# Storing the activated products of two neighbouring table blocks by one transfer in a Hyena, GLA and PEER layer

## The chip, the cores and the metric

The kernel runs on one NeuronCore of a Trainium2 chip. The metric is device time in microseconds (us) of one execution on that core. All data are 32-bit floats; the large products run as float32r matmuls on split operands (a high and a low part), three matmuls for each product.

## The reference, cut to what matters

The layer is computed for 640 tokens: 128 of a prompt and 512 of a sample. The part that matters here is the expert channel mixer at its end. Each token is given 8 x 16 = 128 of 16384 experts; its output is the sum of their rows of a value table, weighted by a gate times the gelu of the token's product with their rows of a key table.

```
    def block(args):
        xt, it, gt = args
        a = jax.nn.gelu(jnp.einsum('td,tkd->tk', xt, u_tab[it]))
        return jnp.einsum('tk,tkd->td', gt * a, v_tab[it])
```

Before it stand the norms, the input projection, the long convolution, the chunked linear attention, the output projection and the product-key search for the 128 experts; the change touches none of them.

## The kernel before, in words

The 640 tokens are five tiles of 128. For three of them (384 tokens, `TA`), the kernel computes the product of every token with every row of the key table `u`, densely, in 128 blocks of 128 table rows, and takes the gelu of it; a dense matrix of gates (zero where an expert is not chosen) later picks what counts. For the two other tiles the chosen rows of `u` are gathered by indirect DMA (`gather_u`, issued by POOL, four buffers `ugat`) and multiplied on DVE (`dot`). Everything goes through DRAM scratch between the two halves: the activated products through `gelu_scratch` (`a_dram`), the gates through `gate_scratch` (`g_dram`).

The dense blocks are numbered n = 0 to 127. For each one:

- SP loads 512 KB of the table into one of four buffers `uraw` (`load_u`), four blocks ahead.
- ACT writes the high part `uhi` (`split_u`), two buffers; POOL (up to block 52) or DVE (after it) writes the low part `ulo`, two buffers.
- PE does 24 matmuls (`first_products`) into one of four PSUM banks.
- ACT takes the gelu from the bank into one of four buffers `aout` (`gelu`), and counts `gelu_done`.
- SP stores the 192 KB of `aout` to `a_dram` (`store_a`), which counts one of the semaphores `a_stored`. Gelu of block n + 4 waits for it, since it writes the same buffer.

SP works strictly in the order of its program: for block n it waits for gelu n, stores, waits for `uhi` and `ulo` of block n, and loads block n + 4. There are three stretches of such blocks. In stretch A (blocks 0 to 51) DVE does the search for the experts beside them. In stretch B (blocks 52 to 115, 64 blocks, `step_b`) PE does eight more matmuls per block that make the gate matrix of 128 tokens from one-hot vectors, ACT copies it to `gst`, and after every eighth block SP stores half of it in two parts of 2048 KB (`store_g`): part 0 right behind block b = 7 or 15 of the sixteen, part 1 behind the store and the load of the next block. Beside this DVE does about 2.8 dots per block up to block 96, two after that, each on a gathered 512 KB. In stretch C (blocks 116 to 127) there are no more gates; DVE does one dot per block, and SP puts in the first four loads of the value table (`load_2`, 512 KB each) and the first read-back of activations and gates (`load_gates(0)`, 768 and 1024 KB, behind block 122). After it stretch D runs the 128 blocks of the second product, 24 matmuls of 512 columns each, for which the activations, gates and value rows are loaded by SP.

All DMAs of SP stand in one queue (q1 of the profile), POOL's gathers in another (q0); both run on the core's 16 DMA engines.

Names and lines: `load_u` L545, `store_a` L549 to L552, `step_a` L558, `store_g` L570, `step_b` L576, stretch C on SP L616 to L632, `first_products` L934 to L951 (its matmuls are L947), ACT's `split_u` L1730 (the activation is L1738), `gelu` L1744, DVE's `dot` L1473 (the operation is L1478), POOL's `gather_u` L1881 (L1886).

Of the kernel before, what the change touches and what calls it, by code (L numbers as in the profile page):

```python
# [127 lines left out]
def bass_hybrid_layer(nc, x, cvec, w_ada, w_in, w_out, w_q, cols, hfcols, hf_w1, hf_w2, hf_w3,  # L128
                      gla_w2, gnorm, state, keys_t, u_t, u_rows, v_tab, zfeat, decay, tab_fwd, tab_inv, tab_p,
                      masks, ident_d, iota_d, out, out_state):  # L130
    a_dram = nc.dram_tensor("gelu_scratch", [P, NBLK, TA], F32, kind="Internal").ap()
# [4 lines left out]
    with ctx:  # L136
        base = 16 * KiB + 256

        def at(name, kib, shape, dt=F32):
            return nc.alloc_sbuf_tensor_at(name, shape, dt, offset=int(base + kib * KiB))  # L140

        def sem(name):
            return ctx.enter_context(nc.semaphore(name))
# [61 lines left out]
        aout = at("aout", 112, [P, 4, TA])  # L205
# [227 lines left out]
        s2_used = sem("s2_used")  # L433
        y_tile = sem("y_tile")
        g_stored = [sem(f"g_stored{b}") for b in range(2)]
        a_stored = [sem(f"a_stored{b}") for b in range(4)]
        u_landed = [sem(f"u_landed{b}") for b in range(4)]
        uhi_ready = sem("uhi_ready")
        ulo_ready = sem("ulo_ready")
# [1 line left out]
        gelu_done = sem("gelu_done")  # L441
# [43 lines left out]
        def _(sp_):  # L485
# [59 lines left out]
            def load_u(n, slot):  # L545
                sp_.dma_start(uraw[:, slot], u_t[bass.ds(n, 1)].rearrange("o p k e -> p (o k) e")
                              ).then_inc(u_landed[slot], 16)

            def store_a(n, slot):  # L549
                sp_.wait_ge(gelu_done, n + 1)  # L550
                sp_.dma_start(a_dram[:, bass.ds(n, 1), :].rearrange("p o t -> p (o t)"), aout[:, slot]
                              ).then_inc(a_stored[slot], 16)  # L552

            wait_unit(sp_, last_unit(loads[-3]))
            for n in range(4):
# [2 lines left out]
            def step_a(it, first):  # L558
                for b in range(4):
                    n = it * 4 + b  # L560
                    store_a(n, b)
                    sp_.wait_ge(uhi_ready, n + 1)
                    sp_.wait_ge(ulo_ready, n + 1)
                    load_u(n + 4, b)
# [32 lines left out]
            def load_2(n):  # L597
                b = n % R2
                if n >= R2:
                    sp_.wait_ge(vhi_ready, n - R2 + 1)  # L600
                    sp_.wait_ge(vlo_ready, n - R2 + 1)
                sp_.dma_start(vraw[b][:], v_tab[n * P:(n + 1) * P, :]).then_inc(v_landed[b], 16)

            def load_gates(m):

                if m >= 2:
                    sp_.wait_ge(w_ready, R2 * (m - 1))
                sp_.dma_start(ain[m % 2][:].rearrange("p i t -> p (i t)"),
                              a_dram[:, R2 * m:R2 * (m + 1), :].rearrange("p i t -> p (i t)")).then_inc(a_landed[m % 2], 16)
                if m >= 2:  # L610
                    sp_.wait_ge(wlo_ready, R2 * (m - 1))
                sp_.dma_start(gin[m % 2][:].rearrange("p c i t -> p c (i t)"),
                              g_dram[:, :, R2 * m:R2 * (m + 1), :].rearrange("c p i t -> p c (i t)")).then_inc(g_landed[m % 2], 16)

            for n in range(BLK_C, NBLK):
                store_a(n, n % 4)  # L616
                if n + 4 < NBLK:
                    sp_.wait_ge(uhi_ready, n + 1)
                    sp_.wait_ge(ulo_ready, n + 1)
                    load_u(n + 4, n % 4)  # L620
                if n == BLK_C + 2:
                    sp_.wait_ge(gate_staged, TD // 4)
                if BLK_C + 2 <= n < BLK_C + 2 + R2:
                    load_2(n - BLK_C - 2)
                if n == BLK_C + 6:
                    for b in range(2):
                        sp_.wait_ge(g_stored[b], 32 * NTD)
                    for b in range(4):
                        sp_.wait_ge(a_stored[b], 16 * (BLK_C // 4))
                    load_gates(0)  # L630
            for b in range(4):
                sp_.wait_ge(a_stored[b], 16 * (NBLK // 4))  # L632

            load_gates(1)
# [930 lines left out]
        def _(act):  # L1565
# [178 lines left out]
            def gelu(n, b, first):  # L1744
                act.wait_ge(h_full, n + 1)
                if not first:
                    act.wait_ge(a_stored[b % 4], (n - b % 4) * 4)
                act.activation(aout[:, b % 4], ps[:, b % 4, 0:TA], ACT.Gelu_apprx_tanh).then_inc(gelu_done, 1)


# [2 lines left out]
            def pair(n, b, first, first_split):  # L1753
                split_u(n + 1, b + 1, first_split)
                gelu(n, b, first)
# [40 lines left out]
            def step_b(it, first):  # L1796
                for b in range(NB_B):
                    n = it * NB_B + b + BLK_A
                    split_u(n + 1, b + 1, False)
                    if n == BLK_A + GELU_U:  # L1800
                        slot_gelu(0)
                    if n + 1 < BLK_C:
                        slot_keys(n + 1 - BLK_A)
                    stage(it, b, first)
                    gelu(n, b, False)
# [189 lines left out]
def build(nc, args):  # L1995
    args[-1] = args[-1].rearrange("b l q h d e -> (b l) q h d e")
    bass_hybrid_layer(nc, *args)
```

## Time and profile before

| | us |
|---|---|
| median of 3 runs | 2192.99 |
| lowest and highest | 2191.74, 2200.29 |
| the profiled execution | 2182.85 |
| its span | 2181.1 |
| stretch A, from about 672 us | 253 |
| stretch B, 925 to 1405 us | 480 |
| stretch C, 1405 to 1472 us | 67 |
| stretch D and the end, from 1472 us | 709 |

The profile is of one execution. It shows each engine's busy time, whom each engine waited for, the time from the issue of a DMA to its landing, the share of time in which the 16 DMA engines were busy, and the clock that TensorE was granted. An engine's idle time costs nothing unless the chain that ends last runs through it, so the stretches are read one by one.

### The profile page before, as it was taken

What the parts mean: (1) busy time and instruction counts of PE and PEld (TensorE: products, weight loads), DVE (VectorE), ACT (ScalarE), POOL (GpSimd) and SP (SyncE); (2) the same over time, 40 slices, a digit from 0 to 9 for tenths busy, and PEclk for the clock granted to TensorE, in tenths of its full rate; (3) what the DMA queues carried; (4) which work ended last, traced back from release to release, by engine and by line L of the source; (5) the groups of instructions that cost most, each with busy time, mean ns of one, the idle gap of its engine ahead of it and who ended that gap; (6) DMA issues with size and microseconds to landing.
All of it is one profiled execution on the core that took longest, in us unless ns stands there. A gap on an engine that the chain in (4) does not pass through costs nothing.

```text
span 2181.1 us, 28455 instructions
## 1 busy us (share of the span) xinstructions
PE 2045.7 (94%) x9877; PEld 1631.1 (75%) x9877; DVE 1522.5 (70%) x3164; ACT 822.2 (38%) x1507; POOL 688.2 (32%) x469
## 2 busy tenths in 40 slices
PE   7999999797998999898888899979999999999998
PEld 3554454645998999887777788878888888888886
DVE  4221415623789999898888888748887687877876
ACT  2111004323212233477777778632222222222222
POOL 0000001003223665433333322224443255545551
PEclk7999999898999999999999999999999999999999
DMA  9121203415112465489999999989999899999994
GB/s 337 66 77 39 83 0 138 173 71 202 40 40 67 155 197 163 144 297 348 348 367 367 343 315 329 334 325 386 380 339 351 292 342 329 345 337 343 336 342 159
DMA packets 183919, 526.01 MB, mean 241 GB/s; under 512 B 16775, under 2 KB 67111, under 8 KB 181256
## 3 DMA queue, kind: packets, MB, share of 16 engines
q1 hardware_dynamic: 128520, 323.41, 40.9%
q0 software_dynamic: 55296, 201.35, 25.7%
q8 instruction: 49, 0.80, 0.1%
q14 instruction: 54, 0.44, 0.1%
HBM read 460.48 MB, written 64.23 MB: 241 GB/s over the span
## 4 chain that ended last, share of the span: by engine, by line
PE 64%; DVE 18%; DMA 9%; issue 5%; ACT 4%; SPq 0%; POOL 0%; ACTq 0%; DVEq 0%
PE ps L1014 32%; DMA ugat<-in_u_rows,idxs 7%; PE ps L664 5%; PE ps L947 4%; DVE junk L1478 3%; PE ps L883 3%; PE ps L757 3%; PE ps L919 3%; PE ps L920 3%; PE ps L723 3%; DVE oneh L1415 2%; PE ps L987 2%; ACT uhi L1738 2%; DVE eA L1496 2%; PE ps L663 1%
## 5 line engine op out<-in xcount | busy, mean ns | idle before, releaser
L947 PE MATMUL ps<-h2hi,uhi 128*128 128x384 f32 x1024 | 399.6, 390 | 32.7 <-issue 19.0
L1886 POOL DMA_INDIRECT ugat<-in_u_rows,idxs x256 | 268.5, 1049 | 512.2 <-DVE dots L1478 501.7
L1014 PE MATMUL ps<-vhi,whi 128*128 128x512 f32 x1024 | 399.1, 390 | 5.1 <-DVE wlo L1525 5.1
L1014 PE MATMUL ps<-vlo,whi 128*128 128x512 f32 x1024 | 399.1, 390 | 0.0
L1014 PE MATMUL ps<-vhi,wlo 128*128 128x512 f32 x1024 | 399.1, 390 | 0.0
L947 PE MATMUL ps<-h2lo,uhi 128*128 128x384 f32 x1024 | 351.3, 343 | 0.0
L947 PE MATMUL ps<-h2hi,ulo 128*128 128x384 f32 x1024 | 349.2, 341 | 0.0
L1816 ACT ACTIVATE vhi<-vraw 128x1024 fp32r<-128x1024 f32 x128 | 135.5, 1061 | 465.8 <-PE ps L1014 445.2
L1894 POOL DMA_INDIRECT vgat<-in_v_tab,idxs x128 | 214.7, 1677 | 222.9 <-DVE y L1536 179.2
L987 PE MATMUL ps<-eA,eB 128*128 128x128 f32 x1024 | 212.2, 289 | 51.9 <-DVE eA L1496 41.0
L987 PEld LDWEIGHTS ps<-eA,eB 128*128 128x128 f32 x1024 | 181.0, 193 | 91.9 <-DVE eA L1496 63.3
L1523 DVE TENSOR_TENSOR vlo<-vraw,vhi 128x1024 fp32r<-128x1024 f32 x128 | 156.7, 1224 | 115.2 <-ACT vhi L1816 115.1
L947 PEld LDWEIGHTS ps<-h2hi,uhi 128*128 128x128 f32 x1024 | 199.5, 195 | 43.6 <-issue 43.0
L1014 PEld LDWEIGHTS ps<-vhi,whi 128*128 128x128 f32 x1024 | 192.7, 188 | 45.8 <-issue 5.8
L1014 PEld LDWEIGHTS ps<-vhi,wlo 128*128 128x128 f32 x1024 | 192.7, 188 | 40.1
L1014 PEld LDWEIGHTS ps<-vlo,whi 128*128 128x128 f32 x1024 | 192.5, 188 | 39.9
L947 PEld LDWEIGHTS ps<-h2lo,uhi 128*128 128x128 f32 x1024 | 199.8, 195 | 0.0
L947 PEld LDWEIGHTS ps<-h2hi,ulo 128*128 128x128 f32 x1024 | 197.9, 193 | 0.0
L1876 POOL TENSOR_TENSOR ulo<-uraw,uhi 128x1024 fp32r<-128x1024 f32 x53 | 141.3, 2666 | 121.7 <-ACT uhi L1738 121.7
L1478 DVE CUSTOM_DVE_ANT_0 junk<-ugat,h2row_u 128x1024 f32<-128x1024 f32 x128 | 155.6, 1216 | 32.5 <-DMA ugat<-in_u_rows,idxs 32.1
L1536 DVE SCALAR_TENSOR_TENSOR y<-vgat,dots,y 128x1024 f32<-128x1024 f32 x127 | 162.7, 1281 | 10.4 <-DMA vgat<-in_v_tab,idxs 4.9
L1478 DVE CUSTOM_DVE_ANT_0 junk<-ugat,h2row_p 128x1024 f32<-128x1024 f32 x128 | 155.9, 1218 | 10.5 <-DMA ugat<-in_u_rows,idxs 9.6
(275 smaller groups left out, 3064.2 us busy)
## 6 DMA issues: line engine op xcount, KB each, us to landing
uraw<-in_u_t SPq DMA_DIRECT2D x128, 512.0 KB, 5.6
vraw<-in_v_tab SPq DMA_DIRECT2D x128, 512.0 KB, 6.9
gate_scratch<-gst SPq DMA_DIRECT2D x16, 2048.0 KB, 13.1
gin<-gate_scratch SPq DMA_DIRECT2D x32, 1024.0 KB, 12.5
wring<-in_w_ada SPq DMA_DIRECT2D x12, 2048.0 KB, 9.4
gelu_scratch<-aout SPq DMA_DIRECT2D x128, 192.0 KB, 4.4
ain<-gelu_scratch SPq DMA_DIRECT2D x32, 768.0 KB, 7.8
wring<-in_w_in SPq DMA_DIRECT2D x6, 2048.0 KB, 8.6
```

The source lines that it names most:

```text
L664: s_ = pe.matmul(bank(us)[0:m], w, as_, start=(j == 0), stop=(j == n - 1))
L723: last = pe.matmul(bank(u), tab[:, t, j, (f - 1) * P:f * P], a(1 + t), start=(t == 0), stop=(t == 3))
L947: last = pe.matmul(ps[:, b % 4, 0:TA], w[:, b % 2, k, :], h[:, k, LP:LP + TA], start=(k == 0 and j == 0), stop=(k == KD - 1 and j == 2))
L987: pe.matmul(o_, eB[:, b % 2, k], eA[:, q % RING], start=True, stop=True).then_inc(onehot_used, 1)
L1014: last = pe.matmul(ps[:, y_bank(t) + h, :], w[:, b, (t - 1) * P:t * P], v[:, b, h * 512:(h + 1) * 512], start=(start and j == 0), stop=(st ...
L1478: dve.tensor_tensor_reduce(junk[:], ugat[:, g % GSLOT], h2row[x][:], 1.0, 0.0, ALU.mult, ALU.add, dots[:, x, k:k + 1]).then_inc(dot_done, 1)
L1523: dve.tensor_tensor(vlo[:, s], vraw[s][:], vhi[:, s].bitcast(F32), ALU.subtract).then_inc(vlo_ready, 1)
L1536: dve.scalar_tensor_tensor(y0[:], vgat[:, s], dots[:, 1, g:g + 1], y0[:], ALU.mult, ALU.add).then_inc(v_added, 1)
L1816: act.activation(vhi[:, s], vraw[s][:], ACT.Copy).then_inc(vhi_ready, 1)
L1876: pool.tensor_tensor(ulo[:, b % 2], uraw[:, b % 4], uhi[:, b % 2].bitcast(F32), ALU.subtract).then_inc(ulo_ready, 1)
L1886: pool.indirect_dma_start(out=ugat[:, g % GSLOT], out_offset=None, in_=u_rows, in_offset=bass.IndirectOffsetOnAxis(ap=idxs[:, g // HK, g % ...
L1894: pool.indirect_dma_start(out=vgat[:, k % GSLOT], out_offset=None, in_=v_tab, in_offset=bass.IndirectOffsetOnAxis(ap=idxs[:, 1, k:k + 1], ...
```

## The change

`store_a` does nothing for an even block. For an odd block n it waits for gelu n, as before, and then stores the blocks n - 1 and n by one transfer: per partition 3072 consecutive bytes in place of 1536, from two neighbouring `aout` buffers to two neighbouring columns of `a_dram`. There is one semaphore for each pair of buffers, so two in place of four, and gelu of block n waits for the store of its pair four blocks back. On SP an even block has no wait for its gelu any more. The bytes stored are the same.

```diff
-        a_stored = [sem(f"a_stored{b}") for b in range(4)]
+        a_stored = [sem(f"a_stored{b}") for b in range(2)]
...
             def store_a(n, slot):
-                sp_.wait_ge(gelu_done, n + 1)
-                sp_.dma_start(a_dram[:, bass.ds(n, 1), :].rearrange("p o t -> p (o t)"), aout[:, slot]
-                              ).then_inc(a_stored[slot], 16)
+                if slot % 2:
+                    sp_.wait_ge(gelu_done, n + 1)
+                    sp_.dma_start(a_dram[:, bass.ds(n - 1, 2), :].rearrange("p o t -> p (o t)"),
+                                  aout[:, slot - 1:slot + 1].rearrange("p o t -> p (o t)")).then_inc(a_stored[slot // 2], 16)
...
                     for b in range(2):
                         sp_.wait_ge(g_stored[b], 32 * NTD)
-                    for b in range(4):
+                    for b in range(2):
                         sp_.wait_ge(a_stored[b], 16 * (BLK_C // 4))
                     load_gates(0)
-            for b in range(4):
+            for b in range(2):
                 sp_.wait_ge(a_stored[b], 16 * (NBLK // 4))
...
                 if not first:
-                    act.wait_ge(a_stored[b % 4], (n - b % 4) * 4)
+                    act.wait_ge(a_stored[b % 4 // 2], (n - b % 4) * 4)
```

PE, ACT, DVE and POOL execute the same instructions in the same order. SP's order changes in two ways that matter. The first place is SP in stretch B, around the end of the first eight blocks of a round. Before, the rows are (L551 is the store of the activations, L546 the load of the table, L573 the two parts of the gates):

```order
L551 DMA gelu_scratch<-aout 128x384 [waits gelu_done]
L546 DMA uraw<-in_u_t 128x1024 [waits ulo_ready,uhi_ready]
L551 DMA gelu_scratch<-aout 128x384 [waits gelu_done]
L546 DMA uraw<-in_u_t 128x1024 [waits ulo_ready,uhi_ready]
L573 DMA gate_scratch<-gst 128x4096 [waits gate_staged]
L551 DMA gelu_scratch<-aout 128x384 [waits gelu_done]
L546 DMA uraw<-in_u_t 128x1024 [waits ulo_ready,uhi_ready]
L573 DMA gate_scratch<-gst 128x4096
L551 DMA gelu_scratch<-aout 128x384 [waits gelu_done]
```

After, at the same place:

```order
L552 DMA gelu_scratch<-aout 128x768 [waits gelu_done]
L546 DMA uraw<-in_u_t 128x1024 [waits ulo_ready,uhi_ready]
L574 DMA gate_scratch<-gst 128x4096 [waits gate_staged]
L546 DMA uraw<-in_u_t 128x1024 [waits ulo_ready,uhi_ready]
L574 DMA gate_scratch<-gst 128x4096
L552 DMA gelu_scratch<-aout 128x768 [waits gelu_done]
L546 DMA uraw<-in_u_t 128x1024 [waits ulo_ready,uhi_ready] x2
```

The wait for a gelu that stood between the two parts of the gates is gone, and elsewhere two loads stand side by side behind one store.

The second place is SP in stretch C, blocks 120 to 123 (`vraw` are the first loads of the value table, `ain` and `gin` the read-back of activations and gates). Before:

```order
L551 DMA gelu_scratch<-aout 128x384 [waits gelu_done]
L546 DMA uraw<-in_u_t 128x1024 [waits ulo_ready,uhi_ready]
L602 DMA vraw_118<-in_v_tab 128x1024
L551 DMA gelu_scratch<-aout 128x384 [waits gelu_done]
L546 DMA uraw<-in_u_t 128x1024 [waits ulo_ready,uhi_ready]
L608 DMA ain_119<-gelu_scratch 128x1536 [waits a_stored1,a_stored2,a_stored0,a_stored3,g_stored1,g_stored0]
L612 DMA gin_121<-gate_scratch 128x8x256
L551 DMA gelu_scratch<-aout 128x384 [waits gelu_done]
L546 DMA uraw<-in_u_t 128x1024 [waits ulo_ready,uhi_ready]
```

After:

```order
L552 DMA gelu_scratch<-aout 128x768 [waits gelu_done]
L546 DMA uraw<-in_u_t 128x1024 [waits ulo_ready,uhi_ready]
L603 DMA vraw_118<-in_v_tab 128x1024
L546 DMA uraw<-in_u_t 128x1024 [waits ulo_ready,uhi_ready]
L609 DMA ain_119<-gelu_scratch 128x1536 [waits a_stored0,a_stored1,g_stored1,g_stored0]
L613 DMA gin_121<-gate_scratch 128x8x256
```

The load of block 126 and the read-back no longer stand behind the gelu of block 122, only behind that of block 121.

## Rows read from the trace of the kernel before

**Rows 1.** The page: shares of the chain that ended last, by line.
```profile
PE ps L1014 32%; DMA ugat<-in_u_rows,idxs 7%; PE ps L664 5%; PE ps L947 4%; DVE junk L1478 3%; PE ps L883 3%; PE ps L757 3%; PE ps L919 3%; PE ps L920 3%; PE ps L723 3%; DVE oneh L1415 2%; PE ps L987 2%; ACT uhi L1738 2%; DVE eA L1496 2%; PE ps L663 1%
```

**Rows 2.** Busy time by stretch: A, B, C, D; PEclk, DMA share, GB/s last.
```profile
core 0: us, PE busy (x) PEld busy (x) DVE busy (x) ACT busy (x) POOL busy (x), PEclk, DMA share, GB/s
660.00:925.00 265.00, 243.37 (x1352) 232.81 (x1350) 245.08 (x715) 88.11 (x127) 144.77 (x57) 0.97 0.47 148
925.00:1405.00 480.00, 427.45 (x2560) 387.49 (x2561) 404.53 (x910) 365.76 (x820) 156.84 (x167) 0.97 0.93 338
1472.00:2181.00 709.00, 698.47 (x3072) 577.77 (x3072) 553.66 (x685) 205.70 (x267) 309.13 (x202) 1.00 0.90 329
```

**Rows 3.** SP's issues in stretch B: two usual blocks, then a gate store.
```profile
941.37 0.35 SPq L551 DMA_DIRECT2D gelu_scratch<-aout  x1
948.29 0.34 SPq L551 DMA_DIRECT2D gelu_scratch<-aout  x1
...
983.75 1.31 SPq L573 DMA_DIRECT2D gate_scratch<-gst  x1
989.80 0.34 SPq L551 DMA_DIRECT2D gelu_scratch<-aout  x1
...
991.21 0.89 SPq L573 DMA_DIRECT2D gate_scratch<-gst  x1
999.82 0.33 SPq L551 DMA_DIRECT2D gelu_scratch<-aout  x1
...
1010.30 0.33 SPq L551 DMA_DIRECT2D gelu_scratch<-aout  x1
```

**Rows 4.** DVE's waits in stretch B: whole, for gathered rows.
```profile
DVE junk L1478 <- DMA ugat<-in_u_rows,idxs: 32.1, 23, 3.5
```

**Rows 5.** Stretch B: DMA share in one usual block and after a gate store.
```profile
941.37:948.29 6.92, 6.48 (x42) 5.88 (x41) 6.75 (x16) 5.80 (x14) 2.81 (x3) 1.00 0.86 317
983.70:991.00 7.30, 6.86 (x44) 6.26 (x44) 7.00 (x16) 6.18 (x16) 3.20 (x4) 1.00 0.95 332
991.00:1001.00 10.00, 7.10 (x36) 6.49 (x35) 6.45 (x15) 5.77 (x15) 2.13 (x3) 0.83 1.01 420
1001.00:1010.00 9.00, 6.46 (x35) 6.14 (x35) 5.49 (x13) 4.31 (x12) 2.71 (x3) 0.86 1.00 415
```

**Rows 6.** Landing times: gate stores of B, then gathers from 925 to 983.7 us.
```profile
DMA to landing us min/median/max: 10.3/13.1/17.0
...
DMA to landing us min/median/max: 5.1/6.0/11.1
```

**Rows 7.** Stretch A: share and GB/s; then first table loads alone; stores' landing.
```profile
810.10:845.80 35.70, 34.86 (x196) 33.29 (x195) 34.08 (x85) 11.65 (x17) 21.18 (x8) 1.00 0.53 168
604.00:612.00 8.00, 8.00 (x60) 8.00 (x59) 7.11 (x35) 1.71 (x3) 2.41 (x1) 1.00 0.72 261
gelu_scratch<-aout SPq DMA_DIRECT2D x9, 192.0 KB, 1.8
```

**Rows 8.** Stretch C on ACT: the splits that waited for a table load.
```profile
1426.83 1.06 ACT L1738 ACTIVATE uhi<-uraw 128x1024 fp32r<-128x1024 f32 x1 [8.43 <-DMA uraw<-in_u_t]
1461.69 1.06 ACT L1738 ACTIVATE uhi<-uraw 128x1024 fp32r<-128x1024 f32 x1 [4.46 <-DMA uraw<-in_u_t]
```

**Rows 9.** Stretch C on SP: the issues of those loads and what stands ahead.
```profile
1407.72 0.88 SPq L573 DMA_DIRECT2D gate_scratch<-gst  x2
...
1410.55 1.06 SPq L546 DMA_DIRECT2D uraw<-in_u_t  x1
...
1446.21 0.68 SPq L612 DMA_DIRECT2D gin<-gate_scratch  x1
...
1449.68 3.25 SPq L546 DMA_DIRECT2D uraw<-in_u_t  x1
```

**Rows 10.** Stretch C: DMA share from 1439 us and after the second late load; PEclk.
```profile
1439.00:1450.00 11.00, 11.00 (x66) 11.00 (x65) 5.63 (x9) 4.33 (x6) 2.81 (x3) 1.00 0.93 333
1462.00:1466.00 4.00, 1.89 (x8) 1.92 (x9) 3.18 (x4) 4.00 (x6) 0.58 (x1) 0.86 0.22 82
```

## The prediction

> **What bounds the kernel now.** I began with the chain of work that ended last and its shares [rows 1]. A third of it is the second product (L1014), 7% are gathered rows, and stores of activations appear nowhere in it: the change takes no link out of the chain itself. It can only act through the DMA engines and through the order of SP's queue. So I read the busy time by stretch [rows 2]. In A the DMA engines are busy 0.47 of the time and DVE's expert search runs 245 of 265 us; DMA is not the limit. In D PE is busy 698 of 709 us. In B the DMA share is 0.93, and this is where the gathered rows stand. In C two splits of ACT waited for a table load [rows 8]. Stretches B and C are where the change can do something.
>
> In B a usual block takes 6.92 us, the distance of two stores [rows 3]; 64 of them would be 443 us, and the stretch is 480. The 37 us more are nearly all DVE's waits for gathered rows, 32.1 us in 23 waits [rows 4], and SP's issues show where: behind a gate store the blocks take 10.0 and 10.5 us [rows 3]. The DMA engines are full there, 1.01 and 1.00 of the time, against 0.86 in a usual block [rows 5]. So outside of the gate stores B is bound by the engines' work, and behind them for some 26 of every 62 us (983.75 to 1010.3; five of the eight gate stores in B have such waits) by the bytes that the DMA engines can move.
>
> **What the change removes.** 64 of 128 stores, each an issue of 0.33 to 0.35 us on SP [rows 3], which mostly waits anyway: nothing. Of DMA time it removes the fixed part of a store. I bound that from stretch A, where nothing contends [rows 7]: a share of 0.53 of 35.7 us over 8.5 blocks of 4.2 us is 2.2 us per block. The first four table loads alone took 0.72 of 8 us, 5.76 us, or 1.44 us each. That leaves some 0.8 us for a store of 192 KB. At the loads' rate per byte it would be 0.54 us, so about 0.29 us is the price of being a small transfer of short rows. One such price goes per pair, whether it hangs on the transfer or on its rows, whose number halves. In B that is 32 x 0.29 = 9.3 us of DMA time. It pays only where the DMA engines are full: 26/62 of it, 3.9 us, less if a late block recovers in the next one. Taken: 4 us gained, with ends of 0 and 9.
>
> The Trainium skill, DMA: Bandwidth & Descriptors, section Bandwidth, has a rule that would promise more: batch transfers to 1 MiB or more, with 0.95 us for 64 KB and 6.15 us for 1 MB. By a line through these two an estimate of the fixed part is 0.6 us, 19 us of DMA time in B and some 8 us of gain by the same share, and the forecast would be 2183. The trace has 0.29 us where it can be read, and I stay with that.
>
> **What it moves in B.** At an even block SP no longer waits for a gelu, and `uhi` and `ulo` of that block are ready by then, since both are made one block ahead. So its load goes out right behind that of the odd block before it, some 6.9 us earlier; two blocks' traffic is issued in one lump of 384 + 512 + 512 KB, then nothing for a block. A load that is earlier helps nobody in B, where ACT waits for no table load. What the lump may hurt is the gathers. In usual blocks they land after 6.0 us in the median [rows 6]; the one of 11.1 us is the last, issued at 983.4 just ahead of the gate store. That one cost DVE a wait of about 2.4 us, so a gather has about 8.7 us before DVE waits. The lump puts 704 KB (0.72 MB) more ahead of some gathers, at most 0.72 / 0.42 = 1.7 us at the full rate [rows 5]: 7.7 us, under 8.7. Taken: 0.
>
> The second part of the gates also goes out earlier, since the wait for a gelu between the parts is gone: at about 985 and not at 991.2 us. That makes the lump 4 MB. But a gate store takes 13.1 us to land, 10.3 at the least [rows 6], and the second part followed the first after 7.5 us [rows 3]: it stood in the queue behind unfinished work already. The engines were busy 0.95 of the time between them [rows 5], so at most 0.05 x 7.3 = 0.4 us of idle DMA time is filled per gate store, 3 us over eight. In turn a moved load (block n + 4 of the even block) falls into the full stretch, 0.5 MB or 1.2 us, and is missing from the block behind it, which was still late too. These go about even. Taken: 0, with ends of 3 us gained and 5 us lost.
>
> **The added wait.** Gelu n of an even block now waits for a store that is issued after gelu n - 3, not n - 4. What is queued behind it on ACT is the split of block n + 2, and PE waits for that. Three blocks are 12.5 us in A and C, 20.7 us in B. Stores land in 1.8 us in A [rows 7]. In C the store of 122 and 123 leaves at 1449 and gelu 126 stands behind the late split of 1461.69 [rows 8], for a load that stands behind this very store in the queue. So the store is done first. Cost 0. The last store is 384 KB in place of 192, at most 0.5 us at the rate of the loads, ahead of the second read-back; it is needed four blocks of 5.5 us later (709 / 128).
>
> **What it moves in C.** The first late load (block 120, wait of 8.43 us) is issued behind the two gate parts, 4 MB [rows 9]. It now leaves at about 1409 in place of 1410.55 us. Ahead of it the 192 KB of block 116 are gone, but those of block 114 have come into the pair that leaves before the gates. Same bytes ahead, same landing: 0 to 1 us gained, taken 0.3. The second late load (block 127, issued at 1449.68, wait of 4.46 us) has the read-back of the gates ahead of it, issued at 1446.21. This now follows block 121 and leaves at about 1443, and the load of block 126 with it. Block 127's load itself stays behind gelu 123. So what gains is only DMA time that was idle between 1439 and 1450 us: 0.07 of 11 us, 0.8 us [rows 10]; with three prices of a small store (0.29) it is 1.7 us. At most it is the whole wait, 4.46 us, and about 1.8 us of a block that PE ran at the lower clock level for part of it after the idle time (0.86 granted there [rows 10]). Taken for C: 2 us gained, ends 0 and 7. What C gains reaches the end, for D begins when the last block is done and PE has no gaps in it [rows 2].
>
> **Sum.** 4 + 0 + 2 = 6 us against the profiled execution: 2182.85 - 6 = 2176.9. The median of the runs lies 10.1 us above that execution, so the predicted time is 2192.99 - 6 = 2187. A measurement of this kernel can tell about 0.5%, 11 us, from no change (2182 to 2204); this is inside.
>
> **The rivals.** *Slower: the lumps make gathers late in usual blocks.* The place is DVE's dot at three per block (blocks 52 to 96, 22 pairs). The point from which it decides is a landing of about 8.7 us. For it: gathers behind a gate store land late at once, so the queue of SP is not harmless to them. Price: 4.19 MB of gates cost 37 / 8 = 4.7 us per store on average, and 7.4 us at the first (3.1 + 3.6 + 0.7 above 6.92), 1.77 us per MB; 0.72 MB x 1.77 x 22 = 28 us if nothing is absorbed, 14 if half is. 2207 to 2221. Against it: 6.0 us of median landing leaves 2.7 us of room. Chance 0.13.
>
> *Faster by far: DMA-full stretches shrink more than in proportion.* If the gate parts side by side and the fewer small stores free a third of B's 37 us, and both waits of C go (8.4 and 4.5 us, with 2 us of clock), it is 12 + 15 = 27 us: 2166; half of this is 2179. For it: shares of 0.86 in usual blocks mean that little is missing for the queue to clear. Against it: the bytes are the same, and nothing leaves the queue ahead of block 120. Chance 0.15.
>
> *Nothing at all:* the stored rows stay 1536 bytes long in the DMA's descriptors, or the fixed part is no occupancy, so B gains 0 and C 1: 2192. Chance 0.17, within the forecast's class.
>
> **How the numbers follow.** Forecast 0.55, nothing 0.17, faster by far 0.15, slower 0.13. Of the forecast's ends (0 to 9, 3 to -5, 0 to 7) the extremes are 2174 and 2198; nearly all of it lies within 11 us of 2193, but 0.02 on the fast side. Faster by over 0.5%: 0.17; within 0.5%: 0.70; slower: 0.13. The range goes from 2176, which takes in half of the fast rival, to 2205, which leaves out the slower one.
>
> **What would show it.** Packets of q1 fall by some 9 thousand (64 stores of 128 rows and 16 semaphore writes). Stretch B: SP's stores 13.8 us apart in usual blocks, loads in pairs, DVE's waits for gathered rows still around 32 us and not in usual blocks; if those waits appear between gate stores, the slower rival is right. Stretch C: the wait of 8.4 us stays, that of 4.5 us falls to about 3. B at 472 to 480 us; if it is below 468, the DMA engines had more to gain than I worked out. ACT must not wait for a store ahead of a gelu.

## The result and the profile after

The changed kernel takes 2195.9 us in the median of 22 runs (2189.8 to 2202.3), the kernel before 2191.3 in 22 runs beside it (2186.6 to 2201.9). The ratio is 1.0018 with a 95% interval of 1.0009 to 1.0026: slower by 4 us, inside the 0.5% that I called no change, but clear of zero and on the other side of the 6 us gained that I forecast. The profiled execution has a span of 2196.2 us against 2181.1.

The page of after, packets and SP's queue:

```profile
DMA packets 174704, 526.00 MB, mean 240 GB/s; under 512 B 15752, under 2 KB 49704, under 8 KB 172041
...
q1 hardware_dynamic: 119304, 323.41, 40.0%
```

SP's queue carries 9216 packets fewer (128520 before), exactly 64 x 128 rows and 64 x 16 semaphore writes, at the same bytes. The change does what it says. SP's issues around the first gate store in after, which answer to [rows 3]:

```profile
973.36 0.34 SPq L552 DMA_DIRECT2D gelu_scratch<-aout  x1
973.80 1.00 SPq L546 DMA_DIRECT2D uraw<-in_u_t  x2
987.19 0.34 SPq L552 DMA_DIRECT2D gelu_scratch<-aout  x1
987.63 1.49 SPq L546 DMA_DIRECT2D uraw<-in_u_t  x1
989.17 0.50 SPq L574 DMA_DIRECT2D gate_scratch<-gst  x1
989.76 0.66 SPq L546 DMA_DIRECT2D uraw<-in_u_t  x1
990.47 0.44 SPq L574 DMA_DIRECT2D gate_scratch<-gst  x1
1001.68 0.34 SPq L552 DMA_DIRECT2D gelu_scratch<-aout  x1
1002.12 0.95 SPq L546 DMA_DIRECT2D uraw<-in_u_t  x2
1024.42 0.34 SPq L552 DMA_DIRECT2D gelu_scratch<-aout  x1
```

Usual pairs of blocks are 13.83 us apart, twice the 6.92 of before. Two table loads leave side by side, and the two gate parts 1.3 us apart and not 7.5. Behind them the pairs take 14.5 and 22.7 us: 9.6 us over the cadence, where before had 7.4 in the same place. DVE's waits for gathered rows in stretch B, after, against [rows 4]:

```profile
DVE junk L1479 <- DMA ugat<-in_u_rows,idxs: 44.0, 26, 4.4
```

44.0 us against 32.1. This is the row that moved most. Dot by dot, 43.8 of the 44.0 us lie in the four blocks that follow the first part of a gate store, as all 32.1 us of before do; usual blocks have next to none in either. Stretch B, with the same windows' columns as [rows 2]:

```profile
928.00:1419.00 491.00, 429.59 (x2564) 388.43 (x2563) 405.08 (x910) 368.17 (x824) 161.34 (x167) 0.97 0.89 331
...
1485.70:2196.00 710.30, 699.98 (x3072) 578.87 (x3072) 554.02 (x685) 205.61 (x267) 311.91 (x202) 0.99 0.90 329
```

From the gelu of block 51 to that of block 115 it is 491.2 us, against 482.8 in the profile of before (four profiles of kernels that run at the speed of before have 482.8 to 488.3, see the table). The DMA engines are less busy (0.89 against 0.93) while DVE waits longer for DMAs. D is as it was. The late table loads of stretch C, against [rows 8]:

```profile
1439.54 1.06 ACT L1739 ACTIVATE uhi<-uraw 128x1024 fp32r<-128x1024 f32 x1 [7.12 <-DMA uraw<-in_u_t]
1442.68 1.06 ACT L1739 ACTIVATE uhi<-uraw 128x1024 fp32r<-128x1024 f32 x1 [1.70 <-DMA uraw<-in_u_t]
...
1474.23 1.06 ACT L1739 ACTIVATE uhi<-uraw 128x1024 fp32r<-128x1024 f32 x1 [5.19 <-DMA uraw<-in_u_t]
```

14.0 us in three waits, against 13.2 in three. C takes 63.8 us from gelu to gelu, before 64.2.

### The profile page after: what moved, and what is told of

Its sections match the earlier page's. It is cut to its first block, busy times and chain, and to the rows that moved or that the text cites. A ratio compares the mean times of both kernels' runs of the same rounds, so it can differ in the third digit from the quotient of the medians.

```text
span 2196.2 us, 28293 instructions
## 1 busy us (share of the span) xinstructions
PE 2043.0 (93%) x9877; PEld 1631.8 (74%) x9877; DVE 1524.7 (69%) x3164; ACT 822.7 (37%) x1507; POOL 693.5 (32%) x469
## 4 chain that ended last, share of the span: by engine, by line
PE 61%; DVE 20%; DMA 12%; issue 4%; ACT 2%; SPq 0%; POOL 0%; ACTq 0%; DVEq 0%
PE ps L1015 32%; DMA ugat<-in_u_rows,idxs 9%; PE ps L665 5%; DVE junk L1479 4%; PE ps L884 3%; PE ps L758 3%; PE ps L920 3%; PE ps L921 3%; PE ps L724 3%; PE ps L948 2%; DVE eA L1497 2%; DVE oneh L1416 2%; DMA wring<-in_w_ada 2%; PE ps L664 1%; DMA uraw<-in_u_t 1%
## 5 line engine op out<-in xcount | busy, mean ns | idle before, releaser
L1887 POOL DMA_INDIRECT ugat<-in_u_rows,idxs x256 | 274.5, 1072 | 518.3 <-DVE dots L1479 506.6
L1015 PEld LDWEIGHTS ps<-vhi,whi 128*128 128x128 f32 x1024 | 193.0, 188 | 45.9 <-issue 5.8
```

Of the source, the lines that this page charges most:

```text
L1015: last = pe.matmul(ps[:, y_bank(t) + h, :], w[:, b, (t - 1) * P:t * P], v[:, b, h * 512:(h + 1) * 512], start=(start and j == 0), stop=(st ...
L1887: pool.indirect_dma_start(out=ugat[:, g % GSLOT], out_offset=None, in_=u_rows, in_offset=bass.IndirectOffsetOnAxis(ap=idxs[:, g // HK, g % ...
```

## The experiments

A table ahead of the details. Ratios are of runs beside before on the same chip; B is the time from gelu 51 to gelu 115 of the one profiled execution, the last column DVE's waits for gathered rows in it (window 925 to 1405 us in all). The four kernels that are no slower than before (before, c1, p1, t3) have B from 482.8 to 488.3 and waits from 31.5 to 32.3 us, which tells how far two single profiles differ.

| kernel | what it has | ratio | 95% | B, us | waits, us |
|---|---|---|---|---|---|
| before, first profile | | | | 482.8 | 32.1 |
| c1 | before, again | 0.9989 | 0.9975 to 1.0004 | 485.5 | 32.2 |
| after | the change | 1.0018 | 1.0009 to 1.0026 | 491.2 | 44.0 |
| e1 | merged stores only | 1.0025 | 1.0013 to 1.0037 | 490.4 | 41.0 |
| e2 | order of after, single stores | 1.0024 | 1.0010 to 1.0038 | 494.0 | 45.5 |
| e3 | after, gelu wait between gate parts | 1.0018 | 1.0004 to 1.0032 | 488.1 | 40.9 |
| e4 | merged, gate parts side by side | 1.0028 | 1.0015 to 1.0042 | 493.6 | 46.5 |
| p1 | before, gelu waits for the pair | 0.9994 | 0.9984 to 1.0005 | 488.3 | 31.5 |
| t1 | stores of 6, 14 held back | 1.0039 | 1.0024 to 1.0054 | 491.0 | 39.9 |
| t2 | the six other even ones held back | 1.0015 | 1.0004 to 1.0027 | 491.5 | 38.6 |
| t3 | early loads only | 1.0000 | 0.9986 to 1.0015 | 487.2 | 32.3 |
| t4 | all even stores held back, single | 1.0055 | 1.0037 to 1.0073 | 495.7 | 45.9 |
| m1 | merged, but 6, 7, 14, 15 alone | 1.0034 | 1.0021 to 1.0046 | 489.8 | 42.4 |
| e6 | before, gates in eight parts | 0.9842 | 0.9825 to 0.9860 | 449.8 | 2.9 |
| m2 | e6 again | 0.9862 | 0.9845 to 0.9878 | 452.1 | 5.2 |
| e7 | after, gates in eight parts | 0.9890 | 0.9871 to 0.9909 | 465.8 | 19.1 |
| s1 | e6, merged stores only | 0.9879 | 0.9853 to 0.9905 | 453.1 | 8.2 |
| s2 | e6, early loads only | 0.9870 | 0.9842 to 0.9898 | 458.1 | 12.2 |
| s3 | e6, held back, single | 0.9902 | 0.9871 to 0.9933 | 469.4 | 22.3 |
| s4 | s1, gate parts sized against the stores | 0.9893 | 0.9862 to 0.9923 | 463.5 | 16.3 |

### Which part of the change costs: e1 to e4

The change does three things to SP's queue: it merges stores, it lets even blocks' loads go early, and it takes the wait from between the gate parts. e1 keeps only the first.

```diff
             def store_a(n, slot):
-                if slot % 2:
-                    sp_.wait_ge(gelu_done, n + 1)
+                sp_.wait_ge(gelu_done, n + 1)
+                if slot % 2:
```

> The changed kernel with one line more: SP again waits for the gelu of an even block ahead of its load, so SP's order is that of before and only the merged store of 384 KB is left of the change. Three theories of the 0.18% lost. Gates: the two 2048 KB parts of a gate store now leave side by side, since no wait for a gelu stands between them, and the gathers are late for longer. Loads: the table loads of even blocks now leave a block earlier, and some fall into the stretch behind a gate store in which the DMA engines are full. Store: the merged transfer itself takes longer turns from the gathers. Gates and loads both expect 0.998 to 1.000 of before here (my estimate of 0.29 us of DMA time saved per pair in B would be 4 us, 0.998, were it right) with DVE's waits for gathered rows in B back at about 32 us; store expects 1.002 again, and waits near 44 us.

Measured 1.0025, with 41.0 us of waits. Neither the loads nor the gate parts are needed for the loss.

e2 takes each merged store apart and keeps the order of after.

```diff
+                    for j in range(2):
+                        sp_.dma_start(a_dram[:, bass.ds(n - 1 + j, 1), :].rearrange("p o t -> p (o t)"),
+                                      aout[:, slot - 1 + j]).then_inc(a_stored[slot // 2], 16)
```

> The changed kernel with each merged store taken apart into two of 192 KB, issued one behind the other at the odd block; SP's order of waits and loads is that of after. Gates and loads: as slow as after or a little more, 1.002 to 1.003 of before. Store: 1.000, since the transfers are those of before.

1.0024, with 45.5 us of waits. With e1 this leaves what both share: the store of the even block leaves a block later than before, and gelu waits for the pair. The theory that the long transfer takes turns from the gathers falls as the whole cause, since e2 has no long transfer.

e3 waits for the even block's gelu ahead of the second gate part alone.

```diff
                     if b == 0 and not first:
+                        sp_.wait_ge(gelu_done, n + 1)
                         store_g(it * 2 - 1, 1, 1)
                     elif b == HALF:
+                        sp_.wait_ge(gelu_done, n + 1)
                         store_g(it * 2, 0, 1)
```

> The changed kernel, with a wait for the gelu of the even block ahead of the second gate part alone; its loads still leave early and the stores are merged. Gates: 0.998 to 1.000 of before, the DMA-full stretches as long as in before. Loads: 1.002, as after.

1.0018, the ratio of after, with 40.9 us of waits. e4 is e1 with the second gate part ahead of the wait.

```diff
                     n = it * NB_B + b + BLK_A
+                    if b == 0 and not first:
+                        store_g(it * 2 - 1, 1, 1)
+                    elif b == HALF:
+                        store_g(it * 2, 0, 1)
                     store_a(n, b % 4)
```

> The changed kernel with the wait for the gelu back at every even block, but the second gate part issued ahead of that wait, right behind the first: gate parts side by side, loads where they were, stores merged. Gates: 1.002 of before. Loads: 0.998 to 1.000.

1.0028, with 46.5 us of waits. By the ratios e4 does not differ from e1, nor e3 from after: the distance of the gate parts is worth nothing that they can tell, as predicted. The waits lean the other way in both pairs: 46.5 us with the parts side by side against 41.0 (e4, e1), and 44.0 against 40.9 (after, e3). With one profile of each that is a hint and no more; a small part of the loss may lie there.

### A control, and the wait on ACT: c1 and p1

> The kernel before, unchanged, run as if it were another: a control. Its ratio should be 1.000 within its interval, and its profile is a second one of before, since the first execution profiled (2182.85 us) was faster than all 22 runs that stood beside after. If the ratio is 1.002 too, the 0.18 to 0.28% of the others is nothing. I expect 1.000, a span near 2190 and some 490 us for stretch B, since e1 to e4 have 488 to 494.

0.9989, its interval takes in 1. With all differences near 0.2% this says how small an effect a dozen runs can tell: 0.1 to 0.15%. Its waits for gathered rows, in the same view as above:

```profile
DVE junk L1478 <- DMA ugat<-in_u_rows,idxs: 32.2, 23, 4.1
```

The first profile had 32.1, and p1 and t3 below have 31.5 and 32.3. So in kernels that run like before the waits repeat well from one execution to the next, and an experiment can be read from them where its ratio alone is too coarse.

p1 keeps every transfer of before in its place and only lets gelu wait for the pair.

```diff
-                              ).then_inc(a_stored[slot], 16)
+                              ).then_inc(a_stored[slot // 2], 16)
...
-                    act.wait_ge(a_stored[b % 4], (n - b % 4) * 4)
+                    act.wait_ge(a_stored[b % 4 // 2], (n - b % 4) * 8)
```

> Before, with its 128 single stores and its order on SP, but with one semaphore for each pair of buffers: gelu of an even block waits for the store of the odd block after it, as in after. All of e1 to e4 have this wait, and all have the store of the even block held back to the odd one. Theory wait: the added wait holds up ACT, 1.002. Theory carried store: the wait costs nothing, 1.000, and what costs is that the store of block 6 or 14, held back, leaves at the start of the DMA-full stretch (0.2 MB at 1.77 us per MB, eight times, 3 us in B).

0.9994 and 31.5 us: the added wait costs nothing (at most 0.05% by the interval). What remains is the store that leaves late.

### Where in B: t1 to t4 and m1

All four t kernels have the single stores of before with their own semaphores, and all edits are in stretch B. t1, t2 and t4 differ in which even blocks' stores are held back until right ahead of the next odd block's.

```diff
+HELD = (6, 14)
...
-            def store_a(n, slot):
+            def store_a(n, slot, hold=False, with_last=False):
                 sp_.wait_ge(gelu_done, n + 1)
-                sp_.dma_start(a_dram[:, bass.ds(n, 1), :].rearrange("p o t -> p (o t)"), aout[:, slot]
-                              ).then_inc(a_stored[slot], 16)
+                for j in ([] if hold else [1, 0] if with_last else [0]):
+                    sp_.dma_start(a_dram[:, bass.ds(n - j, 1), :].rearrange("p o t -> p (o t)"), aout[:, slot - j]
+                                  ).then_inc(a_stored[slot - j], 16)
...
-                    store_a(n, b % 4)
+                    store_a(n, b % 4, b in HELD, b - 1 in HELD)
```

> Before, single stores, waits and loads in place, but in stretch B the stores of blocks 6 and 14 of each sixteen are held back and leave right ahead of those of 7 and 15, that is right ahead of the first gate part. Theory carried store (the cost of the pairing is that 192 KB are carried from a block with room into the start of the stretch in which the DMA engines are full): 1.0015 to 1.0025 of before, DVE's waits for gathered rows near 40 us. Theory lumps (bursts on SP's queue cost wherever they stand): 1.0005.

1.0039, and waits of 39.9 us:

```profile
DVE junk L1480 <- DMA ugat<-in_u_rows,idxs: 39.9, 22, 4.4
```

Two stores of sixteen, moved by one block each, cost 8 us (5 to 12 by the interval), twice what I expected from 0.2 MB.

> Before, with the stores of blocks 0, 2, 4, 8, 10 and 12 of each sixteen held back to the odd block, those of 6 and 14 in place. Carried store: 1.000, waits near 32 us. Lumps: 1.0015 to 1.002.

1.0015 and 38.6 us. The other held stores cost as well; per store the two at the gates cost more (0.39% for two, 0.15% for six, though by the waits, 39.9 and 38.6 us, the two kernels are nearly alike). t2 is no clean opposite of t1: of its six stores those of blocks 0 and 8 would leave between the two parts of a gate store, and held back they leave behind the second. And 36.7 of its 38.6 us of waits still lie in the four blocks behind the first part. So the cost is paid behind the gate stores in both; which of the six stores brings it about isn't shown.

t3 moves the loads alone.

```diff
-                    store_a(n, b % 4)
+                    if b % 2:
+                        store_a(n, b % 4)
                     sp_.wait_ge(uhi_ready, n + 1)
                     sp_.wait_ge(ulo_ready, n + 1)
                     load_u(n + 4, b % 4)
+                    if b % 2 == 0:
+                        store_a(n, b % 4)
```

> Before, with the table load of each even block of stretch B ahead of its wait for the gelu, as in after; stores and gate parts in place. On spread gates this alone cost some 0.3%. Here: between 1.000 (e1, which leaves loads in place, is no faster than after) and 1.002 if early loads cost by themselves.

1.0000 and 32.3 us: early loads are free in this kernel.

> Before, with the stores of all even blocks of stretch B held back, as two transfers each: e1 without the merging. Carried store and lumps both expect 1.002 to 1.003, not under e1's 1.0025, since on spread gates two held stores cost more than a merged one (0.9902 against 0.9879).

1.0055, and the longest waits of all:

```profile
DVE junk L1480 <- DMA ugat<-in_u_rows,idxs: 45.9, 29, 4.4
```

This is twice what I expected, and about the sum of t1 (0.39%) and t2 (0.15%). e1 holds back the same stores of B, in merged form, and costs 0.25%. Side by side t4 and e1 suggest that merging gives back some 0.3%, 6 us; their intervals just touch at 1.0037, and they ran on different chips. But e2 speaks against it: it has no merged store either, holds back every even store, and costs 0.24%, against 0.18% of after, which has the same order on SP. The early loads that e2 has beside t4 cost nothing by t3, but nothing shows that they gain 0.3%. By the waits merging gives back 1.5 us (e2 45.5, after 44.0) or 4.9 us (t4 45.9, e1 41.0). So it may give back something between nothing and 6 us, and how much is not shown.

m1 was the test of the account in which merging gives back 0.3%: merged stores, but nothing carried to the gate parts.

```diff
-            def store_a(n, slot):
-                if slot % 2:
+            def store_a(n, slot, alone=False):
+                if alone:
+                    sp_.wait_ge(gelu_done, n + 1)
+                    sp_.dma_start(a_dram[:, bass.ds(n, 1), :].rearrange("p o t -> p (o t)"), aout[:, slot]
+                                  ).then_inc(a_stored[slot // 2], 16)
+                    return
+                if slot % 2 == 0:
+                    sp_.wait_ge(gelu_done, n + 1)
+                else:
...
-                    store_a(n, b % 4)
+                    store_a(n, b % 4, b % 8 in (6, 7))
```

> e1 (merged stores, waits and loads of before), but the blocks 6, 7, 14 and 15 of each sixteen in stretch B are stored alone, each behind its own gelu, so nothing is carried to the gate parts. If the parts add up: e1's 1.0025, less t1's 0.0039, plus a quarter of what merging gives back (t4 less e1, 0.0030), is 0.9993; range 0.998 to 1.0005. If it stays at 1.002 the carried store is not what costs once stores are merged.

1.0034, and 42.4 us of waits:

```profile
DVE junk L1486 <- DMA ugat<-in_u_rows,idxs: 42.4, 25, 4.1
```

The account of three parts that add up falls. For single stores the place counts: t1 loses 0.39% with two of sixteen stores. In the merged kernel the store carried to the gate parts is not needed for the loss, for without it the loss is no smaller (1.0034 against e1's 1.0025).

### With the bursts gone: e6, e7, s1 to s4, m2

If the waits are bytes that come in bursts, spreading the gate stores must remove them. e6 is before, with parts of 512 KB, one per block.

```diff
-                ii = slice(64 * part_, 64 * part_ + 64)
+                ii = slice(16 * part_, 16 * part_ + 16)
...
-                    if b == 0 and not first:
-                        store_g(it * 2 - 1, 1, 1)
-                    elif b == HALF:
-                        store_g(it * 2, 0, 1)
+                    if b < HALF - 1 and not first:
+                        store_g(it * 2 - 1, 1, b + 1)
+                    elif HALF <= b < 2 * HALF - 1:
+                        store_g(it * 2, 0, b - HALF + 1)
...
-            store_g(NTD * 2 - 1, 1, 1)
...
+                if n < BLK_C + 4:
+                    for part_ in range(2 * (n - BLK_C) + 1, min(8, 2 * (n - BLK_C) + 3)):
+                        store_g(NTD * 2 - 1, 1, part_)
```

> Before, with each gate store of 4 MB in eight parts of 512 KB, one part per block, in place of two parts of 2048 KB. Same bytes. If the 37 us of stretch B are bytes that arrive in bursts on DMA engines that are 0.86 busy otherwise, spreading lets most of them fit in: 10 to 30 us faster, ratio 0.987 to 0.995, DVE's waits for gathered rows well under 32 us. If the waits come from something else, 1.000.

0.9842, 34 us faster, more than I expected. In its profile the waits and the stretches in which before was full [rows 5] read:

```profile
DVE junk L1480 <- DMA ugat<-in_u_rows,idxs: 2.9, 7, 1.1
```

```profile
983.70:991.00 7.30, 6.86 (x44) 6.25 (x45) 7.13 (x18) 6.18 (x15) 3.19 (x4) 1.00 0.83 270
991.00:1001.00 10.00, 9.56 (x62) 8.96 (x61) 9.83 (x23) 7.79 (x17) 4.16 (x6) 1.00 1.01 392
1001.00:1010.00 9.00, 8.45 (x54) 7.56 (x53) 8.68 (x19) 7.88 (x21) 3.67 (x4) 1.00 1.02 404
```

The DMA engines are as full, 1.01 and 1.02, and yet PE does 62 and 54 matmuls in these windows, where before had 36 and 35 (at a granted clock of 0.83 and 0.86 in place of 1.00). Full DMA engines alone are not the trouble; what stands in SP's queue beside the gathers is.

But e6 changes two things at once. A part of 2048 KB is 128 rows of 16384 bytes, a part of 512 KB is 128 rows of 4096. How the two queues share the engines while the second gate part is in flight shows in the profile of before from 1000 to 1005 us (packets, MB, share of the 16 engines; q1 is SP's queue, q0 that of the gathers):

```profile
q1 hardware_dynamic: 106, 1.72, 80.3%
q0 software_dynamic: 108, 0.38, 18.5%
```

The two queues move nearly packet for packet here: beside 105 packets of the gates pass 92 of gathered rows, the rest of the 106 and 108 being semaphore writes of 4 bytes. But a gate packet is 16384 bytes and takes 0.61 us, a gather's is 4096 bytes and takes 0.16 us, so the gathers get a fifth of the engines, 0.38 MB in 5 us. In e6 no packet of the gates is longer than a gather's, and from 991 to 1001 us, with the engines full, the shares are:

```profile
q0 software_dynamic: 560, 2.07, 53.7%
q1 hardware_dynamic: 598, 1.85, 47.0%
```

In before the gathers move 1.51 MB in that window. So there is a rival to the spreading: the shorter rows alone may give much of the 34 us. No run keeps the two large parts and shortens their rows, so which of the two it is stays untested.

e7 is after with the same edit.

> The changed kernel with the same spread gate stores. Carried store and all theories in which the change costs through the DMA-full stretches: the difference between after and before disappears, e7 within 0.1% of e6. Theory wait: e7 stays 0.2% above e6.

0.9890, 9 us above e6, and 19.1 us of waits. The loss did not vanish with the gate bursts; it grew. A cost that needs the two large gate parts falls. A cost that needs full DMA engines does not, for in e6 they are busy 0.98 of the time from 928.5 to 1370 us, and no block has room. s1 to s3 take the change apart on this base.

> e6 (gate stores in eight parts) with the merged stores and pair semaphores, and SP's waits and loads where they are in before. e7, the whole change on spread gates, is 9 us slower than e6 in the medians and 16 us in the profiles' stretch B, with DVE's waits for gathered rows at 19.1 against 2.9 us. Theory lump of stores: the block in which 384 KB of stores leave has more bytes than the DMA engines move in a block of 6.92 us; it expects 7 to 9 us above e6 here. Theory loads: 0 to 2 us.

> e6 with single stores, each behind its own gelu, but the table load of an even block ahead of that block's wait for the gelu, as in after: the loads move, the stores do not. Theory lump of stores: 0 to 2 us above e6. Theory loads: 7 to 9 us above e6.

> e6 with the store of each even block held back and issued right ahead of that of the odd block, as two transfers of 192 KB with rows of 1536 bytes; waits, loads and semaphores as in e6. Against s1 it shows what merging itself does. Theory lump: equal to s1. If the longer rows of the merged transfer are what takes turns from the gathers: near e6 here and slow in s1.

s1 changes `store_a` as e1, s2 as t3 (in all stretches), s3 as t4:

```diff
                 sp_.wait_ge(gelu_done, n + 1)
-                sp_.dma_start(a_dram[:, bass.ds(n, 1), :].rearrange("p o t -> p (o t)"), aout[:, slot]
-                              ).then_inc(a_stored[slot], 16)
+                if slot % 2:
+                    for j in range(2):
+                        sp_.dma_start(a_dram[:, bass.ds(n - 1 + j, 1), :].rearrange("p o t -> p (o t)"), aout[:, slot - 1 + j]
+                                      ).then_inc(a_stored[slot - 1 + j], 16)
```

Measured 0.9879, 0.9870 and 0.9902, waits of 8.2, 12.2 and 22.3 us, against 0.9842 to 0.9862 and 2.9 to 5.2 of e6 and its repeat. Lump and loads each had one kernel that was to be slow; both were a little slow, so neither theory alone is right here. By the waits, one profile each, held single stores cost most, early loads less, and the merged store least, 3 to 5 us over e6 and m2. The ratios are coarser: s3 and e7 stand clear of e6 (up to 0.9860), but their intervals begin at 0.9871 and that of m2 ends at 0.9878, so no kernel of this group stands clear of both.

s4 tries whether the bytes per block are what counts: gate parts of 320 KB at odd and 704 KB at even blocks.

```diff
-                ii = slice(16 * part_, 16 * part_ + 16)
+                ii = slice(32 * (part_ // 2) + (10 if part_ % 2 else 0), 32 * (part_ // 2) + (32 if part_ % 2 else 10))
```

> s1 with gate parts of unequal size: 320 KB at odd blocks, where the 384 KB of stores leave, and 704 KB at even blocks, so that each block sends out about the same number of bytes (1216 KB). Theory lump: back to e6 within 2 us, DVE's waits for gathered rows near 3 us. If the merged transfer or the held store costs for another reason: as slow as s1.

0.9893 and 16.3 us: no better than s1. Equal bytes per block do not bring e6 back. The edit also changed the length of the gate rows (2560 and 5632 bytes against 4096), so it does not rule out the bytes cleanly. The rows of the larger parts became longer than a gather's 4096 bytes, which the rival above would make a cost.

> e6 unchanged (before, with the gate stores in eight parts of 512 KB, single stores), a second time on another chip or day beside m1: the version that beats both kernels. 0.984 again, within 0.982 to 0.986.

0.9862, a little outside what I expected: some 31 us, 1.4%. The version that beats both kernels has single stores.

## Why the prediction was wrong, point by point

**The price of a small store** is the first step that failed. I took 0.29 us of DMA time per pair as saved, 4 us in B. In stretch A, where nothing contends, the share of SP's queue from 702 to 910 us reads, for c1, e1 and after in this order:

```profile
q1 hardware_dynamic: 13205, 33.06, 48.8%
```

```profile
q1 hardware_dynamic: 9968, 33.27, 49.3%
```

```profile
q1 hardware_dynamic: 9936, 33.17, 45.9%
```

e1 has the merged stores and a quarter fewer packets at the same share: the saved occupancy is nil. The lower share of after comes with SP's order (e2, single stores in that order, has 47.0). The packets themselves say where my term came from. In that window a row of 1536 bytes takes 65 ns in the mean in c1 and one of 3072 bytes 132 ns in e1, so a store of 192 KB is 128 x 65 / 16 = 0.52 us of DMA time, what its bytes cost at the loads' rate, and a merged pair is 1.06 us. What was longer is the table loads: a row of 4096 bytes takes 215 ns in before, 1.72 us a load, and not the 1.44 us of the first four. I had put the loads' extra time down to the stores. (My own figures, 2.23 less 1.44 less 0.54, give 0.25 us and not 0.29, which changes little.) In B a row of 3072 bytes takes 122 ns against 65, so merging saves 0.06 us a pair, 2 us of DMA time in 32 pairs where I had 9.3. In time it may give something back there (e1 against t4, s1 against s3), but e2 against after shows next to nothing, and it is in no case as much as holding the store back costs. The page's rule that I weighed beside it, larger batches (the Trainium skill, DMA: Bandwidth & Descriptors, Bandwidth), promised more than my term, and the row of e1 speaks against it at this size. The figures in that section of the Trainium skill are of loads issued from GpSimd; these are stores issued from SP.

**The lump and the gathers** is the second, and it set the sign. I asked whether two blocks' traffic makes gathers late in usual blocks, found 7.7 us under the 8.7 that a gather has, and took 0. For the usual blocks that was right: in after nearly all stand at 13.83 us per pair, and 0.2 us of waits are there. But I never asked what the held store does behind a gate store, where gathers are late already and every further delay is paid in full. There the late blocks grew, and DVE's waits went from 32 to 44 us. That the held store does it is shown by t1, t2 and t4, which hold back single stores and change nothing else, and lose 0.15 to 0.55%. I had the price in hand (1.77 us per MB) and used it only for the rival. Even that is too low: t1 moves 0.2 MB per gate store, eight times, 1.6 MB in all, and pays 8 us, 5 us per MB.

**The slower rival** had the sign, the queue and the victim right, and the place and the sum wrong: 14 to 28 us in usual blocks, against 4 measured, and nearly all the waits behind the gate stores. I gave it 0.13.

**The moved loads and gate parts** in B: taken 0, measured 0 within what the ratios can tell (t3: 1.0000; e3 against after, e4 against e1: no difference). The waits of e4 and of after, 3 to 6 us longer than those of e1 and e3, leave room for a small cost of the gate parts, inside the 5 us that I allowed.

**The added wait:** taken 0, measured 0 (p1: 0.9994).

**Stretch C:** taken 2 us gained. In the profiles it is 63.8 against 64.2 and, in c1, 65.2 us; the wait of block 127's load did not fall to 3 us but stayed at 5.2 (4.5 and, in c1, 5.1). The read-back left earlier, but that load found the queue no emptier: ACT could start on it 13.0 us after its issue, before 12.0. 0 to 1 us gained, of which I can't say more.

**Sum by the runs:** B loses some 5 us in the profiles (491.2, against 482.8 to 488.3 where nothing is held back), C nothing clear, 4 us in all by the medians; I had minus 4, and minus 2. The time lies inside my range, 2176 to 2205, but that is no merit of the account: the range was wide enough for either sign.

**What stays open.** Why 192 KB that wait one block cost so much. It isn't bytes (none are added), isn't ACT's wait (p1), isn't the loads (t3). The place counts for single stores (t1), but with merged ones the loss stays when the stores at the gates are left alone (m1), so it is no plain sum of parts. It would fit that a store put ahead of a load or a gate part changes what the gathers share the engines with, and the packets above show that the sharing depends on what SP's queue holds. But no run here changes that alone, and I leave it at that.

## What to carry to other kernels

Before merging two transfers, ask what the first of them waits for: what is saved per transfer can be less than what it costs to send the first one later, and that is dearest where a queue is full already. A stretch whose DMA engines are 0.86 busy but whose work stops behind each large transfer wants that transfer cut up and spread over the blocks, in rows no longer than those of the transfers beside it; here the two together were worth 1.4 to 1.6%, where the merging was worth less than nothing. And an effect of 0.2% is better read from one repeated row (a wait in total: 31.5 to 32.3 in four kernels without it, 38.6 to 46.5 in nine with it) than from medians alone, though differences inside the second group are not to be trusted to 2 or 3 us.

## What the runs showed that I had not expected

The first profile of before was of a lucky execution, and part of its 10 us under the median lies in a place that the change can't reach. PE's granted clock from 404 to 414 us, in the linear attention, was 0.86 in that execution and 0.50, the lower level, in after and in p1:

```profile
404.00:414.00 10.00, 10.00 (x70) 9.18 (x70) 4.51 (x12) 4.14 (x18) 0.00 (x0) 0.86 0.11 40
```

```profile
404.00:414.00 10.00, 10.00 (x41) 8.83 (x41) 2.90 (x6) 2.07 (x9) 0.00 (x0) 0.50 0.09 35
```

The first row is of before, the second of after. 70 matmuls against 41 in the same 10 us put all later work some 3 us back. In both PE had just waited 6.6 us for DVE. The control had 0.91. So two profiles of the same kernel can differ by more than this change does, and only stretch against stretch, with a control beside them, were they comparable.

The second is that full DMA engines need not hold up anything: e6 ran them at 1.01 and 1.02 with PE at its usual pace, where before, at 1.01 and 1.00, did some three fifths of the matmuls. What the gathers got of them from 991 to 1001 us differed, 2.07 MB in e6 and 1.51 MB in before.
